# Matrix-memory attention with keys on the partitions: the running maximum from doubling steps on a row, the decay straight from ScalarE, row sums from a column of ones

## The reference, cut to what matters

```python
qk = jax.nn.silu(causal_dwconv(jnp.concatenate([q_m, k_m], axis=-1), conv_w, conv_b))
ig = (i_m + b_igate)
lf = jax.nn.log_sigmoid((f_m + b_fgate))
...
d_mat = b_c[..., :, None] - b_c[..., None, :] + ig_[..., None, :]     # b_c: cumulative sum of lf
d_mat = jnp.where(causal, d_mat, -jnp.inf)
inter = b_c + m_s[..., None]
m_row = jnp.maximum(inter, jnp.max(d_mat, axis=-1))
s_mat = jnp.einsum('bhtd,bhsd->bhts', q_, k_) * jnp.exp(d_mat - m_row[..., None])
...
h = num / jnp.maximum(jnp.abs(den), jnp.exp(-m_row))[..., None]
...
hm = rms_norm_2(hm, mlstm_out_norm) * sigmoid(o_m)
```

## Time and profile before

| what | value |
|---|---|
| runs of before | median 4042.66 us of 3 (4034.44 to 4046.18) |
| the profiled execution | 4041.36 us |
| its span | 4039.6 us |
| mean granted TensorE clock | 0.893 of full |
| TensorE busy | 3460.7 us, 86% of the span |
| VectorE busy | 1845.0 us, 46% |
| ScalarE busy | 1060.0 us, 26% |
| GpSimd busy | 2.7 us |
| DMA | 336.65 MB, mean 83 GB/s |

### The profile page before, as it was taken

The page is one execution under the profiler, slowest core; times in us unless marked ns, Lnnn a source line. Parts: engine busy times, 40 slices in busy tenths (PEclk is TensorE's granted clock), DMA queues, the critical chain, the costliest instruction groups (busy, mean ns, idle before and its releaser), DMA issues. The chain is left out here.

```text
span 4039.6 us, 49005 instructions
## 1 busy us (share of the span) xinstructions
PE 3460.7 (86%) x20184; PEld 2896.6 (72%) x20184; DVE 1845.0 (46%) x3591; ACT 1060.0 (26%) x1709; POOL 2.7 (0%) x8
## 2 busy tenths in 40 slices
PE   5997998999997978989996945679997983678997
PEld 4987786888886967878776934468885972456886
DVE  3224554333335235544435466653334547655333
ACT  2112443111112232432222223332222322423222
POOL 0000000000000000000000000000000000000000
PEclk7996898999998987999998977589998995779999
DMA  5440101423231211144452300025543320012332
GB/s 188 130 138 1 46 26 49 132 78 118 87 120 55 74 45 35 43 125 137 150 162 86 96 21 1 0 73 162 160 132 122 92 62 0 1 42 79 98 95 73
DMA packets 318718, 336.65 MB, mean 83 GB/s; under 512 B 12024, under 2 KB 233760, under 8 KB 318368
## 3 DMA queue, kind: packets, MB, share of 16 engines
q1 hardware_dynamic: 318496, 333.52, 27.0%
HBM read 329.80 MB, written 3.67 MB: 83 GB/s over the span
## 5 line engine op out<-in xcount | busy, mean ns | idle before, releaser
L1323 DVE TENSOR_TENSOR weights_low<-weights,weights_high 128x1024 fp32r<-128x1024 f32 (+4 forms) x424 | 485.4, 1147 | 1289.0 <-ACT weights_high L989 1287.2
L989 ACT ACTIVATE weights_high<-weights 128x1024 fp32r<-128x1024 f32 (+4 forms) x424 | 422.2, 998 | 1429.0 <-PE banks L513 991.3
L889 PE MATMUL banks<-h_high,weights_high 128*128 128x512 f32 (+1 forms) x1760 | 658.6, 374 | 12.3 <-DVE h_low L1335 11.1
L889 PE MATMUL banks<-h_low,weights_high 128*128 128x512 f32 (+1 forms) x1760 | 649.6, 369 | 0.0
L889 PE MATMUL banks<-h_high,weights_low 128*128 128x512 f32 (+1 forms) x1760 | 648.5, 368 | 0.0
L513 PE MATMUL banks<-weights_high,h_high 128*128 128x426 f32 (+3 forms) x1424 | 519.9, 365 | 19.1 <-DVE h_low L1335 19.1
L513 PE MATMUL banks<-weights_high,h_low 128*128 128x426 f32 (+3 forms) x1424 | 511.7, 359 | 0.0
L513 PE MATMUL banks<-weights_low,h_high 128*128 128x426 f32 (+3 forms) x1424 | 511.4, 359 | 0.0
L889 PEld LDWEIGHTS banks<-h_high,weights_high 128*128 128x128 f32 x1760 | 332.7, 189 | 86.0 <-DVE h_low L1335 19.2
L889 PEld LDWEIGHTS banks<-h_high,weights_low 128*128 128x128 f32 x1760 | 332.7, 189 | 55.9
L889 PEld LDWEIGHTS banks<-h_low,weights_high 128*128 128x128 f32 x1760 | 332.9, 189 | 52.0
(11 more groups left out here) (247 smaller groups left out, 3879.8 us busy)
## 6 DMA issues: line engine op xcount, KB each, us to landing
projected<-in_w_mod SPq DMA_DIRECT2D x80, 1024.0 KB, 5.2
weights<-in_w_gate_up SPq DMA_DIRECT2D x88, 512.0 KB, 3.9
weights<-in_w_down SPq DMA_DIRECT2D x80, 512.0 KB, 4.2
weights<-in_w_in SPq DMA_DIRECT2D x80, 426.0 KB, 3.4
weights<-in_w_gate SPq DMA_DIRECT2D x44, 512.0 KB, 6.6
weights<-in_w_up SPq DMA_DIRECT2D x44, 512.0 KB, 7.7
weights<-in_w_mod SPq DMA_DIRECT2D x32, 512.0 KB, 3.9
weights<-in_w_out SPq DMA_DIRECT2D x32, 512.0 KB, 3.6
```

Of the source, the lines that this page charges most:

```text
L889: mm = pe.matmul(bank[:, 0:cnt], wt[:, k, :], x[:, k, a:a + cnt], start=(k == 0 and q == 0), stop=(k == KD - 1 and q == 2))
L989: act.activation(WH[s_ % 2][:, 0:k * n], slots[j % LAND][:, 0:k * n], ACT.Copy).then_inc(S["w_high"], 1)
L1323: dve.tensor_tensor(WL[s_ % 2][:, 0:k * n], slots[split_of[s_] % LAND][:, 0:k * n], WH[s_ % 2][:, 0:k * n].bitcast(F32), ALU.subtract).the ...
```

## The change

The units run over (head, key tile s) with keys on the partitions and queries 128 s to 511 along the row, so the weighted scores come out as TensorE needs them for the value product; the turns and their copies go.

- **Maximum.** i(s) - b(s) stays a column per key tile (`T16`). Its row form is clamped at 0 into `TOP` (4 rows of 512, with 256 zeros ahead), and nine steps of max(x[t], x[t - 2^k]) make M(t) for all four heads. TensorE turns M back to columns (L857 of the new kernel); DVE adds b, and ACT takes one exp of 16 columns: the floor for all units.
- **Decay.** TensorE copies M's row onto 128 partitions once per head (`tops`, new L673). DVE adds +1e30 where the query is earlier than the key in the four diagonal blocks, one instruction for a head (`masked`, new L1478). ACT takes exp(-M + (i - b)) with the key's column as bias: the diagonal block from the masked copy (new L1085), the other columns straight from PSUM (new L1087). DVE multiplies by scale and scores (`prob`, new L1488).
- **Row sums.** The values lie in `VA` with a column of ones as 129th; the value product (new L690) gives numerator and denominator. GpSimd fills `VA` when softmax attention is done. One `output` per head (new L1495 to L1499) works on four query tiles at once.
- **Order.** The Sigmoid, and Exp and Ln of the forget gate, stand ahead of the convolutions on ACT; the sums and turns of the gates stand between the turns of slices 4 and 6; Silu is applied slice by slice.
- The constants lose 384 columns of the causal mask and gain 128 of the new one (256 columns less).

```diff
+        TOP = [SC[0:4, 5200 + 768 * i:5968 + 768 * i] for i in range(2)]
+        PTT = [SC[:, 8784 + 1280 * i:10064 + 1280 * i] for i in range(2)]
+        VA = SC[:, 11344:11344 + 2064].rearrange("p (t h e) -> p t h e", t=4, e=129)
+        OUT = [PSA[:, 2048 + 1024 * i:3072 + 1024 * i].rearrange("p (n e) -> p n e", e=256) for i in range(2)]
+        ml_units = [(h, s_) for h in range(ML_H) for s_ in range(LAT_T)]
+        ml_at = [0, 512, 896, 1152]
@@ TensorE @@
+                def tops(h):
+                    if h >= 2:
+                        pe.wait_ge(S["ml_exp"], 4 * (h - 1))
+                        pe.wait_ge(S["ml_masked"], h - 1)
+                    pe.matmul(PS[h % 2], CN[0:4, C_SEL + 128 * h:C_SEL + 128 * (h + 1)], TOP[1][:, 256:768],
+                              start=True, stop=True).then_inc(S["ml_tops"], 1)
+
+                def scores(g):
+                    h, s_ = ml_units[g]
+                    if g >= 2:
+                        pe.wait_ge(S["ml_prob"], g - 1)
+                    pe.matmul(PS[2 + g % 2][:, 0:512 - 128 * s_], QK[:, 4 + h, 128 * s_:128 * (s_ + 1)], QK[:, h, 128 * s_:512],
+                              start=True, stop=True).then_inc(S["ml_scores"], 1)
+
+                def values(g):
+                    h, n = ml_units[g]
+                    pe.wait_ge(S["ml_prob"], g + 1)
+                    if h >= 2 and n == 0:
+                        pe.wait_ge(S["ml_out"], h - 1)
+                    for s_ in range(n + 1):
+                        at = ml_at[s_] + 128 * (n - s_)
+                        mm = pe.matmul(OUT[h % 2][:, n, 0:129], PTT[h % 2][:, at:at + 128], VA[:, s_, h, :], start=(s_ == 0), stop=(s_ == n))
...
+                tops(0)
+                scores(0)
+                for g, (h, s_) in enumerate(ml_units):
+                    if s_ == 0 and h + 1 < ML_H:
+                        tops(h + 1)
+                    if g + 1 < len(ml_units):
+                        scores(g + 1)
+                    if g == 0:
+                        pe.wait_ge(S["v_ones"], 2)
+                    values(g)
+                pe.wait_ge(S["ml_out"], ML_H)
...
-                for f in range(8):
+                for f in range(4):
...
+                for f in range(4, 6):
+                    turn_columns(lambda t: pr(t, M_Q + 128 * f, 128), ["a"])
...
+                for f in range(6, 8):
+                    turn_columns(lambda t: pr(t, M_Q + 128 * f, 128), ["a"])
+                pe.wait_ge(S["row_tops"], 1)
+                bank = B.fill(pe, "d")
+                for n in range(LAT_T):
+                    mm = pe.transpose(bank[:, 4 * n:4 * n + 4], TOP[1][:, 256 + n * PT:256 + (n + 1) * PT], ident[0:4, 0:4])
+                mm.then_inc(S["filled"], 1)
@@ GpSimd @@
+                pool.wait_ge(S["mix_out"], group_of(units, len(units) - 1) + 1)
+                pool.memset(VA[:, :, :, 128:129], 1.0).then_inc(S["v_ones"], 1)
+                pool.tensor_copy(VA[:, :, :, 0:128], PW[:, :, M_V:M_V + 512].rearrange("p t (h e) -> p t h e", e=128)).then_inc(S["v_ones"], 1)
@@ ScalarE @@
+                    if s_ == 0:
+                        act.wait_ge(S["ml_tops"], h + 1)
+                        act.wait_ge(S["ml_masked"], h + 1)
+                    if g >= 2:
+                        act.wait_ge(S["ml_prob"], g - 1)
+                    n, key = 512 - 128 * s_, T16[:, s_, h:h + 1]
+                    ins = act.activation(DT[g % 2][:, 0:128], MD[h % 2][:, 128 * s_:128 * (s_ + 1)], ACT.Exp, scale=-1.0, bias=key)
+                    if n > 128:
+                        ins = act.activation(DT[g % 2][:, 128:n], PS[h % 2][:, 128 * (s_ + 1):512], ACT.Exp, scale=-1.0, bias=key)
+                    ins.then_inc(S["ml_exp"], 1)
...
+                og = PW[:, :, M_O:M_O + 512]
+                act.activation(og, og, ACT.Sigmoid).then_inc(S["gate_act"], 1)
                 roots(LAT_T * ATT_H)
+                act.wait_ge(S["abs_f"], 1)
+                step(act.activation(T16[:, :, :], T16[:, :, :], ACT.Exp, scale=-1.0))
+                act.activation(T16[:, :, :], T16[:, :, :], ACT.Ln, bias=ones_col).then_inc(S["ln_f"], 1)
+
+                def conv_silu(f):
+                    act.wait_ge(S["conv"], f + 1)
+                    act.activation(QK[:, f, :], QK[:, f, :], ACT.Silu).then_inc(S["conv_silu"], 1)
...
-                act.activation(SC[:, 0:4096], SC[:, 0:4096], ACT.Silu).then_inc(S["conv_silu"], 1)
...
+                    if f:
+                        conv_silu(f - 1)
+                conv_silu(7)
...
+                act.wait_ge(S["floor"], 1)
+                act.activation(IG, LF, ACT.Exp, scale=-1.0).then_inc(S["floor_exp"], 1)
@@ VectorE @@
+                def masked(h):
+                    dve.wait_ge(S["ml_tops"], h + 1)
+                    if h >= 2:
+                        dve.wait_ge(S["ml_exp"], 4 * (h - 1))
+                    dve.tensor_tensor(MD[h % 2].rearrange("p (s q) -> p s q", s=4), PS[h % 2].rearrange("p (s q) -> p s q", s=4),
+                                      CN[:, C_LATE:C_LATE + 128].unsqueeze(1).broadcast_to([PT, 4, PT]), ALU.add).then_inc(S["ml_masked"], 1)
+
+                def prob(g):
+                    h, s_ = ml_units[g]
+                    n = 512 - 128 * s_
+                    dve.wait_ge(S["ml_scores"], g + 1)
+                    dve.wait_ge(S["ml_exp"], g + 1)
+                    if h >= 2 and s_ == 0:
+                        dve.wait_ge(S["ml_values"], 4 * (h - 1))
+                    dve.scalar_tensor_tensor(PTT[h % 2][:, ml_at[s_]:ml_at[s_] + n], PS[2 + g % 2][:, 0:n], float(np.float32(128 ** -0.5)),
+                                             DT[g % 2][:, 0:n], ALU.mult, ALU.mult).then_inc(S["ml_prob"], 1)
+
+                def output(h):
+                    dve.wait_ge(S["ml_values"], 4 * (h + 1))
+                    if h == 0:
+                        dve.wait_ge(S["floor_exp"], 1)
+                    step(dve.tensor_copy(rs[:, 0:4], OUT[h % 2][:, :, 128]))
+                    step(dve.scalar_tensor_tensor(rr[:, 0:4], rs[:, 0:4], -1.0, rs[:, 0:4], ALU.mult, ALU.max))
+                    step(dve.tensor_tensor(rr[:, 0:4], rr[:, 0:4], IG[:, :, h], ALU.max))
+                    step(dve.reciprocal(rr[:, 0:4], rr[:, 0:4]))
+                    dve.tensor_tensor(PW[:, :, M_Q + 128 * h:M_Q + 128 * (h + 1)], OUT[h % 2][:, :, 0:128],
+                                      rr[:, 0:4].unsqueeze(2).broadcast_to([PT, 4, PT]), ALU.mult).then_inc(S["ml_out"], 1)
+
+                masked(0)
+                for g, (h, s_) in enumerate(ml_units):
+                    prob(g)
+                    if s_ == 2 and h + 1 < ML_H:
+                        masked(h + 1)
+                    if s_ == 1 and h:
+                        output(h - 1)
+                output(ML_H - 1)
...
+                conv(0)
                 dve.wait_ge(S["ln_f"], 1)
                 dve.tensor_tensor(LF, LF, T16, ALU.subtract).then_inc(S["log_forget"], 1)
+                for f in range(1, 4):
+                    conv(f)
                 bank = B.empty(dve, "d", "d")
                 dve.tensor_copy(BC.rearrange("p t h -> p (t h)"), bank[:, 0:16]).then_inc(S["emptied_dve"], 1)
                 dve.wait_ge(S["emptied_dve"], B.emptied_by("d"))
                 dve.tensor_tensor(T16, IG, BC, ALU.subtract).then_inc(S["gate_cols"], 1)
+                conv(4)
+                conv(5)
                 bank = B.empty(dve, "d", "d")
-                copy_out(bank[0:4, :], CT)
+                dve.tensor_scalar(TOP[0][:, 256:768], bank[0:4, :], 0.0, None, ALU.max).then_inc(S["emptied_dve"], 1)
+                dve.wait_ge(S["emptied_dve"], B.emptied_by("d"))
+                for k in range(9):
+                    x = TOP[k % 2]
+                    step(dve.tensor_tensor(TOP[1 - k % 2][:, 256:768], x[:, 256:768], x[:, 256 - 2 ** k:768 - 2 ** k], ALU.max))
+                dve.sem_inc(S["row_tops"], 1)
+                conv(6)
+                conv(7)
+                bank = B.empty(dve, "d", "d")
+                dve.tensor_tensor(LF.rearrange("p t h -> p (t h)"), BC.rearrange("p t h -> p (t h)"), bank[:, 0:16], ALU.add).then_inc(S["emptied_dve"], 1)
+                dve.wait_ge(S["emptied_dve"], B.emptied_by("d"))
+                dve.sem_inc(S["floor"], 1)
```

114 lines of the change are left out of this document (17 added, 97 removed).

## The result

| what | before | after |
|---|---|---|
| median of the runs | 4043.89 us of 4 (4034.44 to 4046.18) | 3970.39 us of 4 (3967.28 to 3975.33) |
| the profiled execution, its span | 4041.36, 4039.6 us | 3969.1, 3967.3 us |
| TensorE busy | 3460.7 us | 3395.9 us |
| VectorE busy | 1845.0 us | 1801.2 us |
| mean granted clock | 0.893 | 0.902 |

The account below looks back on a forecast made before the run. Units bound by TensorE's fp32 products at half clock, by the DVE, ACT, DVE, PE exchange at full. Start at 3502.5 plus 33.8 us of units saves 32.8 us a layer, 65.6 in all: 3977 us, range 3962 to 4000.

Parts of the forecast that it names:

- The first convolution, 3.2 us lost: Ahead of the convolutions: Exp and Ln before ACT's copies make DVE begin at 3475.8 instead of 3472.6, 3.2 us lost.
- Eight convolutions on DVE's 2.23 us, ACT below it: Convolutions: DVE stays the bound at 2.23 us each, ACT's copies and sliced Silu taking 2.0 us.
- Sums and turn hidden: Gates: TensorE's 4.43 us of sums lie under convolutions 1 to 3, the 1.01 us turn under 4 and 5.
- The running maximum, 7.3 us: Before the last convolutions: one instruction and nine dependent 4x512 steps, wholly on DVE's path, 7.3 us.
- Units all at full clock, 29.2 us: The 16 units: TensorE's 25.5 us, 2.1 held up by outputs and 1.6 for the last output give 29.2 us.
- The output's hold: In the units: the output between two multiplications holds TensorE about 0.7 us for three heads, 2.1 at full clock.
- The clock's rise, 10 us in, cost 4.6: In the units: TensorE's clock rises after 10 us at half level, losing 4.6 us, so units take 33.8 us.
- the "nothing" for the constants: Program start: 256 fewer columns of constants gain nothing, since the first modulation tiles outlast that transfer.
- Early clock: Rival for the units: full level after about 5 us, costing 2.3 instead of 4.6; 31.5 us, total 3972; chance 0.20.
- Half clock to the end: Rival for the units: half clock throughout, 48.9 us, a gain of 17.7 a layer, total 4007; chance 0.17.
- The exchange rival: Units: exponentials, multiplication, value product and signals run serially, about 2.5 us a unit, 41.6 us, total 3993; chance 0.13.
- GpSimd's copy: Value copy after attention: about 2 us, hidden, DVE's norm not slowed; rival that the first value product waits, chance 0.04.

Follow-up runs that it names:

- E10: The change with Exp and Ln of the forget gate behind ScalarE's copies of the first slice instead of ahead of them: 3974.3 us, ratio 0.9834.
- E1: The kernel before with only the new order of gates, convolutions and Silu, and the old units: 4041.4 us, ratio 1.0013.
- E3: The change with nineteen dependent maximum steps instead of nine, the ten more altering nothing: 3985.8 us, one execution.
- E5: The change with 45 unread identity turns ahead of TensorE's wait for the running maximum and 30 more ahead of the units: 3962.4 us, ratio 0.9828.
- E11: The change with one scan, later output, Exp and Ln behind the first slice's copies, and added identity turns: 3951.6 us, ratio 0.9783.
- E7: The change with a head's output two multiplications later in VectorE's list: 3963.8 us, ratio 0.9818.
- E9: The change with its four row products made over 128 rows instead of 4, the further rows zero: 3964.4 us, one execution.
- E2: The kernel before with the units' row products made over 128 rows instead of 4: 4024.8 us, one execution.
- E8: The change with the constants as wide as before, 256 more columns that nothing reads: 3978.7 us, ratio 0.9855.
- E4: The change with GpSimd's copy of the values held until VectorE has formed |z| of the gates: 3978.3 us, one execution.
- E6: The change with one scan in place of the nine maximum steps: 3962.4 us, ratio 0.9817.
- E12: The change with one scan, later output, Exp and Ln behind the first slice's copies, and row products over 128 rows: 3952.3 us, ratio 0.9783.

## Why the prediction was right, term by term

*The first convolution, 3.2 us lost:* 3.1 (13.9 us behind the start of the stretch, 10.8 before). E10 names the cause, Exp and Ln ahead of the copies, and shows that 1.4 of it can be had back.

*Eight convolutions on DVE's 2.23 us, ACT below it:* 2.24, without a gap. *Sums and turn hidden:* they are; E1 confirms the balance of the new order at 2.3 us a layer.

*The running maximum, 7.3 us:* 7.2, all of it on the path (E3). *First row product:* forecast 40.7 us behind the start, measured 40.3.

*Units all at full clock, 29.2 us:* 28.4 (E5). Two errors largely cancel in it, and so far the closeness is luck. TensorE's own work, forecast 25.5, is 23.8 (E11: 25.3 less the last output's 1.5). The term that was too dear is the scores: they were scaled from the 1.05 us of a product with 4 rows to 2.9 us a head, and take 2.4 (in E11 the widest takes 0.86 us to the start of the next product). The output's hold was mis-sized the other way: forecast 2.1 us for three heads, measured 3.2 (E7). The 0.7 in that term was DVE's surplus over TensorE's cover; behind the five instructions of the output the value product really came 0.96 us late (1.18 us behind the start of the scores ahead of it, against 0.22 in E7).

*The clock's rise, 10 us in, cost 4.6:* 9.5 us in, cost 4.3 (E5). That it would rise and stay was right, with a reason that the runs bear out in part: of "fewer 4-row products and no waits", E9 and E2 show that making these products over 128 rows moves the rise from 9.5 to 6.0 us in the new units and from 13.9 to 3.8 in the old ones; the waits were not tested by themselves. The 10 us were a choice between 13.5 and 5 that nothing in the prediction worked out. It came out close by luck: starting the units 1.4 us earlier (E10) put the rise at 11.0 us.

*Sum:* 34.3 us a layer against 32.8 forecast, 68.5 against 65.6. The remaining 4 us between the two profiled executions lie within the spread outside the stretches (3821 to 3841 us); the "nothing" for the constants stands but for a microsecond or so that E8 can't exclude.

*The rivals.* Early clock: the rise came later than its 5 us; the Trainium skill's rule, that activity releases the throttle (page "TensorE: Matmul & The Clock Gate", section on the HAM clock gate), doesn't tell apart the 13.9, 9.5 and 6.0 us that before, the change and E9 needed with TensorE busy all the time. Half clock to the end did not happen. The exchange rival (2.5 us a unit, 41.6 in all) falls with E11: 16 units and the last output in 25.3 us, bound by TensorE. GpSimd's copy took 4 instead of 2 us, and had 44 us to spare; DVE's norm lost nothing by it, so the 0 taken for that term was right (E4).

## What to carry to other kernels

Put the bookkeeping of a finished head behind the instruction that the bound engine waits for next, not ahead of it: here the five instructions of an output, 1.4 us in DVE's list, cost TensorE a pause three times a layer, and moving one call gave 3.2 us a layer back. Ask for each dependent chain of short steps whether one instruction does it (a scan took 1.21 us where nine steps took 6.38). And when effects of a few us are to be told apart in a run of 4000, time the stretch between two fixed instructions: it repeated within 0.1 us where the totals moved by 10.

## What was not expected of the hardware

- The rows of a product bear on when TensorE's clock rises, and on how long the product and the next one take. With 128 rows (124 of them zeros) instead of 4, the rise came 6.0 instead of 9.5 us behind the first product (E9), and the old units ran at 0.79 to 0.86 instead of 0.62 (E2). At full clock a row product of 512 columns and the scores of 384 behind it took 1.51 instead of 1.80 us (E9). Turns of an identity raised the clock too: in E5 it fell at 3455.0 and was up again at 3458.4 with nothing but turns in between.
- An earlier start of the units was followed by a later rise: 11.2 us at 0.50 when they began 5.2 us earlier (E6), 11.0 when 1.4 earlier (E10), and 9.0 when 7.2 later (E3). With 128 rows this was not seen: 5.7 us with a start 6.6 us earlier (E12) against 6.0 (E9). The cause is open.
- A GpSimd copy of 128x2048 took 1.89 us alone and 3.97 when it began just behind a DVE multiplication of 2.29 us (E4); DVE lost nothing.
- The same 100 us of the attention of layer one ran at 0.70 to 0.86 of the clock from execution to execution, and a run at 0.70 was 10 us behind one at 0.82 when layer two began.
